# The expert stage's choice of width: compares in one block at the loop's head instead of a nested tree

## What is computed

```
top_val, top_idx = lax.top_k(tok @ w_router, 2)
xs = tok[token_of]                      # tokens sorted by expert
g = lax.ragged_dot(xs, w_gate, group_sizes)
u = lax.ragged_dot(xs, w_up, group_sizes)
y = lax.ragged_dot(jax.nn.silu(g) * u, w_down, group_sizes)
```

## Time and profile before

| what | value |
|---|---|
| device time, median of 3 runs | 4548.6 us (4547.06 to 4548.66) |
| span of the profiled execution | 4554.2 us |
| PE busy (share) | 3869.1 us (85%) |
| PEld busy | 3520.6 us (77%) |
| DVE / ACT / POOL busy | 2316.3 / 1755.4 / 829.9 us |
| expert stage, from its first product to the output phase | about 1795 to 4500 us |

### The profile page before, as it was taken

The page is one execution under the profiler, slowest core; times in us unless marked ns, Lnnn a source line. Parts: engine busy times, 40 slices in busy tenths (PEclk is TensorE's granted clock), DMA queues, the critical chain, the costliest instruction groups (busy, mean ns, idle before and its releaser), DMA issues. The chain is left out here.

```text
span 4554.2 us, 65309 instructions
## 1 busy us (share of the span) xinstructions
PE 3869.1 (85%) x23414; PEld 3520.6 (77%) x23415; DVE 2316.3 (51%) x3372; ACT 1755.4 (39%) x2324; POOL 829.9 (18%) x319
## 2 busy tenths in 40 slices
PE   5988867999999573869979979979699897997993
PEld 3964455777777452869979979978699897997993
DVE  2347733545545423756644444458444486454554
ACT  5146613322322132545433333345333354443442
POOL 0000000111111202322222112223222132221222
PEclk8988878999999786989989989999899998998996
DMA  4136634322322324655544444446443465444544
GB/s 166 34 131 222 222 105 171 102 92 92 108 95 65 140 113 98 225 174 185 184 129 133 138 137 135 134 154 229 138 154 132 135 221 178 157 138 137 175 166 178
DMA packets 433346, 662.95 MB, mean 146 GB/s; under 512 B 33361, under 2 KB 348881, under 8 KB 432977
## 3 DMA queue, kind: packets, MB, share of 16 engines
q1 hardware_dynamic: 413026, 587.84, 38.8%
q0 software_dynamic: 15776, 55.61, 3.4%
q10 hardware_dynamic: 4176, 15.21, 0.8%
HBM read 599.32 MB, written 59.29 MB: 145 GB/s over the span
## 5 line engine op out<-in xcount | busy, mean ns | idle before, releaser
L1822 POOL TENSOR_TENSOR moe_d_lo<-moe_raw_d,moe_d_hi 128x2048 fp32r<-128x2048 f32 x126 | 582.9, 4626 | 1947.3 <-ACT moe_d_hi L1962 1947.3
L2132 DVE SCALAR_TENSOR_TENSOR moe_y_t<-moe_y,moe_cols,moe_y_t 128x256 f32<-128x256 f32 (+3 forms) x936 | 480.7, 533 | 181.8 <-PE moe_y L1873 176.9
L1871 PE MATMUL moe_g<-moe_x,moe_g_hi 128*128 128x352 f32 (+3 forms) x1344 | 421.3, 313 | 145.0 <-issue 145.0
L2079 DVE TENSOR_TENSOR moe_g_lo<-moe_raw_g,moe_g_hi 128x2048 fp32r<-128x2048 f32 x127 | 359.2, 2829 | 214.2 <-ACT moe_g_hi L1962 212.9
L1872 PE MATMUL moe_g<-moe_x,moe_g_hi 128*128 128x352 f32 (+3 forms) x1344 | 421.0, 313 | 6.5 <-issue 6.5
L1873 PE MATMUL moe_g<-moe_x,moe_g_lo 128*128 128x352 f32 (+3 forms) x1344 | 420.1, 313 | 0.0
L1871 PE MATMUL moe_y<-moe_h,moe_d_hi 128*128 128x352 f32 (+3 forms) x1344 | 417.7, 311 | 1.3 <-DVE moe_y_t L2132 1.1
L1872 PE MATMUL moe_u<-moe_x,moe_u_hi 128*128 128x352 f32 (+3 forms) x1344 | 415.7, 309 | 0.0
L1872 PE MATMUL moe_y<-moe_h,moe_d_hi 128*128 128x352 f32 (+3 forms) x1344 | 415.7, 309 | 0.0
L1873 PE MATMUL moe_u<-moe_x,moe_u_lo 128*128 128x352 f32 (+3 forms) x1344 | 415.6, 309 | 0.0
L1873 PE MATMUL moe_y<-moe_h,moe_d_lo 128*128 128x352 f32 (+3 forms) x1344 | 415.5, 309 | 0.0
(11 more groups left out here) (317 smaller groups left out, 9509.7 us busy)
## 6 DMA issues: line engine op xcount, KB each, us to landing
moe_raw_g<-in_moe_w_gate SPq DMA_DIRECT2D x127, 1024.0 KB, 5.6
moe_raw_u<-in_moe_w_up SPq DMA_DIRECT2D x127, 1024.0 KB, 5.0
moe_raw_d<-in_moe_w_down SPq DMA_DIRECT2D x126, 1024.0 KB, 4.9
att_w_mod<-in_w_ada SPq DMA_DIRECT2D x20, 2048.0 KB, 8.6
scratch_y<-att_zeros SPq DMA_DIRECT2D x11, 2048.0 KB, 14.1
ffn_raw_g<-in_ffn_w_gate SPq DMA_DIRECT2D x22, 1024.0 KB, 5.5
ffn_raw_u<-in_ffn_w_up SPq DMA_DIRECT2D x22, 1024.0 KB, 5.4
ffn_raw_d<-in_ffn_w_down SPq DMA_DIRECT2D x22, 1024.0 KB, 4.9
```

The source lines that it names most:

```text
L1822: pool.tensor_tensor(d_lo[par][:, :, :], raw_d[:, :, :], d_hi[par][:, :, :].bitcast(F), ALU.subtract)\
L1871: pe.matmul(bank[:, 0:width], wh, moving[:, 0, 0:width], start=start, stop=False)
L2079: dve.tensor_tensor(lo[par][:, :, :], raw[:, :, :], hi[par][:, :, :].bitcast(F), ALU.subtract).then_inc(split, 1)
L2132: dve.scalar_tensor_tensor(y_t[:, db, 0:cols], y_ps[db % 4][:, 0:cols], gate, y_t[:, db, 0:cols], ALU.mult, ALU.add).then_inc(y_added, 1)
```

## The change

The head of the loop, all compares and the loop's end now lie in one block of some 22 instructions, ahead of all widths' programs. A compare jumps straight to a width's program, or falls to the next compare; the program of width 128 follows right behind the block. Each program ends with one jump to the loop's end (`tail`), which adds to the counter and jumps to `head`. Only when all 11 passes are done does the engine jump over all programs to the end of the stage. A pass without work goes from the first compare to the tail. SP, POOL and the dense layer keep `each_pass` or the plain list of passes. The loops inside a width's program and the work in it are the same; at the widths used they lie 3 to 13 instructions further on.

```
-        def each_width(eng, width_no, body):
+        def each_width(eng, who, body):
...
-            def among(first, last):
...
-                    width = WIDTHS[first - 1]
-                    body(width, 2 * width < TOKENS - 2 * ROUND)
...
-                with eng.If(width_no <= middle):
-                    among(first, middle)
-                    eng.nop()
-                with eng.If(width_no > middle):
-                    among(middle + 1, last)
-                    eng.nop()
...
+                with nc.body(node(first, last), valid_engines=this):
+                    if last - first > 1:
+                        eng.br_cond(width_no <= middle, on_true=node(first, middle), on_false=node(middle + 1, last))
+                    else:
+                        eng.br_cond(width_no <= first, on_true=node(first, first), on_false=f"{node(first, last)}_else")
...
+            nc.regs_mov(counter, 0)
+            nc.br(head, engines=this)
+            with nc.body(head, valid_engines=this):
+                p = nc.snap(counter, min_val=0, max_val=passes - 1)
+                width_no = eng.value_load(table[0:1, 1, bass.ds(p, 1)], min_val=0, max_val=len(WIDTHS))
+                eng.br_cond(width_no <= 0, on_true=tail, on_false=node(1, len(WIDTHS)))
+                tree(1, len(WIDTHS))
+                with nc.body(tail, valid_engines=this):
+                    nc.regs_add(counter, counter, 1)
+                    nc.br_lt(counter, passes, on_true=head, on_false=f"{end}_far", engines=this)
+                with nc.body(f"{end}_far", valid_engines=this):
+                    eng.br(end)
+                for k, width in enumerate(WIDTHS):
+                    with nc.body(node(k + 1, k + 1), valid_engines=this):
+                        body(p, width, 2 * width < TOKENS - 2 * ROUND)
+                        eng.br(tail)
+            nc.switch_bb(end)
...
-            each_pass(pe, one_pass)
+            each_width(pe, "pe", one_pass)
...
-            each_pass(act, one_pass)
+            each_width(act, "act", one_pass)
...
-            each_pass(dve, one_pass)
+            each_width(dve, "dve", one_pass)
```

More of the change, by code:

```diff
@@ L1723, in each_pass @@
                 for p in range(passes):
-                    body(p, None)
+                    body(p)
                 return
@@ L1728, in each_pass, with node, tree @@
                 with eng.If(width_no > 0):
-                    body(p, width_no)
+                    body(p)
                     eng.nop()
-        def each_width(eng, width_no, body):
-            if width_no is None:
-                body(TOKENS, False)
+        def each_width(eng, who, body):
+            if table is None:
+                for p in range(passes):
+                    body(p, TOKENS, False)
                 return
-            def among(first, last):
+            this = bass.OrderedEngineSet([eng.engine])
+            counter = nc.alloc_registers(f"{name}_{who}_pass", engines=this)
+            head, tail, end = (f"{name}_{who}_{at}" for at in ("head", "tail", "end"))
+            def node(first, last):
+                return f"{name}_{who}_widths_{first}_{last}"
+            def tree(first, last):
@@ L1753, in each_width @@
-            eng.nop()
+                with nc.body(node(first, last), valid_engines=this):
[3 more added lines that the diff above has]
+                        eng.br_cond(width_no <= first, on_true=node(first, first), on_false=f"{node(first, last)}_else")
+                if last - first == 1:
+                    with nc.body(f"{node(first, last)}_else", valid_engines=this):
+                        eng.br(node(last, last))
@@ new lines, in tree @@
+                tree(first, middle)
+                tree(middle + 1, last)
+            nc.regs_mov(counter, 0)
[14 more added lines that the diff above has]
+                        eng.br(tail)
@@ L1797, in expert_of, with one_pass @@
                 return sp.value_load(table[0:1, 0, bass.ds(p, 1)], min_val=0, max_val=gate_w.shape[0] - 1)
-            def one_pass(p, _):
+            def one_pass(p):
                 expert = expert_of(p)
@@ L2009, in ready_tokens @@
                     act.activation(x[:, k, 0, :], x_full[:, k % 2, :], ACT.Copy).then_inc(x_rounded, 1)
[L2011 to L2044, removed]
@@ new lines, in one_pass, with step @@
+            def one_pass(p, width, narrow):
+                def step(c, par, round_next=True):
+                    if round_next:
+                        round_g(p, c + 1, 1 - par)
+                    silu(p, c, 0, width, narrow)
+                    if round_next:
+                        round_u(p, c + 1, 1 - par)
+                    round_hidden(p, c, par, 0, width)
+                    silu(p, c, 1, width, narrow)
+                    round_hidden(p, c, par, 1, width)
+                    round_d(p, c, par)
+                chunk_pairs(act, p, 0, C - 2, step)
+                step(C - 1, parity(p, C - 1), has_next(p))
+                if has_next(p):
+                    ready_tokens(p + 1)
+                tiles = -(-width // P)
+                for t in range(TILES_PASS):
+                    if t < tiles:
+                        act.wait_ge(y_turned, p * KD + 2 * t + 1 + T0)
+                        act.wait_ge(y_stored[t % 2], (p * (TILES_PASS // 2) + t // 2 + 1) * 16)
+                        act.activation(y_out[:, t % 2, 0:D // 2], y_ps[2 * t % 4][:, :], ACT.Copy)\
+                           .then_inc(y_left, TILES_PASS - tiles + 1 if t == tiles - 1 else 1)
+                        act.wait_ge(y_left, p * TILES_PASS + t + 1 + O0)
+                        act.wait_ge(y_right, p * TILES_PASS + t + 1 + O0)
+                        act.dma_start(y_rows(p, t), y_out[:, t % 2, :]).then_inc(y_stored[t % 2], 16)
+                    else:
+                        act.wait_ge(y_stored[t % 2], (p * (TILES_PASS // 2) + t // 2 + 1) * 16)
+                        act.sem_inc(y_stored[t % 2], 16)
```

127 lines of the change are left out of this document (61 added, 66 removed).

## The result

The changed kernel takes 4413.6 us (4404.9 to 4422.4, four runs), the kernel before beside it 4548.6 (4547.1 to 4554.4): a ratio of 0.9706, 95% interval 0.9690 to 0.9721. That is 135 us less; 95 were forecast. A later comparison of the same two kernels (five and nine runs) gave 4416.8 against 4547.4, 130.6 us less, ratio 0.9706 (0.9693 to 0.9720). The direction held, the size did not, and the time lies outside the forecast range.

What follows compares the result with a forecast made beforehand. PE's idles between passes, 172.1 us of far-jump fetches, were taken as the bound; 91.0 us there plus 4.1 at the stage's end save 95.1, so 4554.2 becomes 4459.1, less 5.6 for the median: 4454 us, range 4440 to 4482.

Steps and rivals of the forecast that it cites:

- the block was not cut: Rival: a border between code pieces cuts the compact block, head and tail need a fetch each; 39 us less saved, 4493; chance 0.08.
- no inner loop fetched in its rounds: Rival, slower: a moved inner loop of ACT or DVE crosses a border and fetches each round; 216 us, 4670; chance 0.03.
- the exits of passes of width 128 and 160 were kept: PE's exits from narrow passes cost no fetch; the rival, every exit a fetch, 14.7 us less saved, 4469, chance 0.22.
- With one fetch I take 12.4 less 4.9 [...], 7.5 us.: PE's idle at a change with one fetch: the shortest earlier idle less the median jump back; after passes 0, 3, 4, 6.
- lost through the wide ones: PE's instruction memory loses the compact block during wide passes, so their exits fetch and four changes have two fetches.
- two fetches at 12.4: PE's idle at each of four changes with two fetches, taken as 12.4 us from an idle in the earlier trace.
- The end of the stage: ACT's way out after the last pass: exit, empty passes and one far jump, 4.1 us saved.
- ACT's corrections: Taken off PE's sum because ACT is late: 0.2 us at pass 1, 1.4 us after pass 3; 92.6 becomes 91.0.
- several us to spare: Outside passes 1 and 7 and the narrow passes, ACT was taken to have several us in hand before PE needs the weights.
- ACT sets the pace: Rival: ACT's walk paces every change, 17 fetches of 4 us, 68 + 4.1 us saved, 4477; chance 0.13.
- What else moves costs nothing: Counter, work in the programs, and order of SP's and POOL's loads and gathers stay the same; 0 us.
- The clock: PE's granted clock may stay up, or exits start earlier, at short idles: up to 2 us at four changes, 8 us, left out.

Runs made afterwards that it cites:

- tail_far: The changed kernel with PE's tail (count and jump back) behind all programs, as in the kernel before; 4453.5 us.
- exit_waits: The changed kernel, but PE's sequencer waits for its last transposes of a pass before it takes the exit; 4438.1 us.
- after_again: The changed kernel once more, unchanged; 4416.8 us, ratio 0.9706 to the kernel before.
- own_all: The changed kernel with a count, table read and compares of its own behind every program on PE, ACT and DVE; 4404.9 us, ratio 0.9684.

## Why the prediction was right in direction and wrong in size

**What held.** The idles are fetches at far jumps; tail_far puts ten more such fetches in and gets 44 us of idle and 40 us of time. The tail costs 0.2 us, the block was not cut, no inner loop fetched in its rounds, ACT did not set the pace, and the exits of passes of width 128 and 160 were kept. The terms of PE were the right terms: each of the eight idles shrank.

**The step that failed first: "With one fetch I take 12.4 less 4.9 [...], 7.5 us."** Measured are 4.46, 3.97 and 4.59 us after passes 0, 4 and 6, and 5.69 into the 128 of pass 4: 11.3 us over four changes. The 12.41 of the earlier trace rows is a poor measure in two ways. Taking off the jump back leaves in it the exit of 5.97 us, where entries after the change took 3.7 to 4.2 us in most changes. And its lead is as short as any: its first far jump starts 1.0 us ahead of the end of the transposes (3017.0, the idle beginning at 3018.0), while after the change the exits start 1.1 to 3.6 us ahead, and where the exit is kept all of the lead goes into the entry's fetch. I named this with "up to 2 us at four changes" and left it out of the sum. exit_waits prices the lead at 21.3 us over eight changes, 2.7 each; 1.0 of each was in my measure, so some 13 us over the eight were not, by this estimate.

**The second: the block "lost through the wide ones".** Behind passes 1 and 5 it was kept, so that two changes for which I took 12.4 us had 2.67 and 7.29, 14.8 us. I had reasoned from six packets in a wide pass and two at its entry. From the exit ahead of pass 1 to that after it the trace after shows 7 packets of q8; so it does through pass 2, whose exit was lost (windows 2006 to 2263 and 2265 to 2602.6 us). Through pass 5 (3173.1 to 3512) it was 4, presumably since part of 352's code was still there from pass 3. The rows of these three windows, and that of pass 0 (1785 to 2004.5):

```profile
q8 instruction: 7, 0.11, 0.2%
...
q8 instruction: 7, 0.11, 0.2%
...
q8 instruction: 4, 0.07, 0.1%
...
q8 instruction: 3, 0.05, 0.1%
```

The number of packets does not decide it alone. Counting every place as new in each wide pass was the error at pass 5.

**The third: two fetches at 12.4.** They were 10.53 and 10.07, and 11.2 in after_again: 4.2 us for the two. The three parts make 11.3 + 14.8 + 4.2 = 30.3, the 30.2 us that were missing.

**The end of the stage** gave 6.6 and not 4.1 us. **ACT's corrections** (0.2 at pass 1, 1.4 in the narrow passes) had the wrong place for the first: PE waited for the low parts 1.9 and 1.6 us in pass 4, where the 1.6 stood before the change as well, and 0.3 us in pass 2, and not at pass 1. That DVE hangs on ACT was read rightly, but that both have "several us to spare" elsewhere was true of the shortened walks only: with the old ones PE waits in seven passes. The rival "ACT sets the pace" was closer than its 0.13 says: it became true as soon as ACT kept its tree.

**"What else moves costs nothing"** did not hold either: the 6.5 us of second stops in the passes of 352 went away. It didn't show in the sum, since as much came back: the stage length less the idles is 2507.5 us before and 2506.9 after.

**The clock**, which I had left out: over the first 10 us of the eight passes the mean granted clock was 0.74 of full speed before and 0.79 after, part of it perhaps because the second stops were gone. The first product after the shortest idle (2.67 us) took 0.42 us instead of 0.66, the other seven took 0.57 to 0.66, much as before. No gain of the size that I allowed for is seen in the passes' own length.

The sum: the span lost 143.3 us and not 95.1. Of the 48.2 between them, 30.2 are PE's idles, 1.6 ACT's corrections that didn't come where I put them, 2.5 the end of the stage, 11.5 the chance ahead of the stage, and 2.4 the second stops (6.5) less what came back elsewhere (4.1). Without the chance 36.7 are left, and the longer comparison misses 35.5 (130.6 less 95.1).

## What to carry to other kernels

Price a far jump as a fetch, then subtract what the sequencer's lead and the waits around it cover, place by place: an idle taken from the place with the shortest cover overstates what will remain at the others. Where several engines walk the same branches side by side, shorten all the walks at once; one alone gives nothing or half (here 0 to 3, 65, and 131 to 135 us for ACT with DVE, for PE, and for all three). Putting a fetch ahead of work that others wait for only moves the idle; a copy of the choosing code behind each program removes the way back altogether.

## What the runs showed of the hardware that I had not expected

PE's instruction memory kept a block through programs of 256 and 352. Neither "oldest out" nor "longest unused out" with one fixed size fits what was seen. By age: the block came in anew at the exit of pass 2 and was lost at that of pass 3, 8 packets later; it came in anew there and was kept until the exit of pass 6, 15 packets later. By last use: 7 packets lay between two uses in pass 1, where it was kept, and 7 in pass 2, where it was lost. The first two counts (2609.5 to 2951.9 and 2957 to 3738 us):

```profile
q8 instruction: 8, 0.13, 0.2%
...
q8 instruction: 15, 0.25, 0.1%
```

The Trainium skill (Runtime: NRT & Kernel Launch, "Instruction fetch mechanics") describes PE's as a FIFO of 128 KiB filled in blocks of 16 KiB, which makes eight blocks, and beside it two cache lines. After the block at the head had come in, 3 packets came in pass 0 and 7 up to the exit of pass 1, ten in all, and that exit took 0.30 us; here the measurement speaks against both descriptions. What decides between keeping and losing stays open.

Kernels with the same work ahead of it reached the expert stage at times from 1779.4 to 1799.4 us in 17 profiled executions of 16 kernels, and the changed kernel itself at 1783.6 and 1791.9. This is a scatter of 0.4% of the time, more than most differences between the versions above, and only a length measured inside the stage tells them apart.

On ACT a far jump does not show in the branch. ACT's branches of the choice took 34 to 50 ns in the changed kernel, whether they led far or not, and the stop lies behind them as an idle put down to "issue". What one costs ACT is known only as a bound: in own_all, with a single way to walk, ACT's idle behind the passes of three tiles was 2.93, 5.45, 5.23 and 5.57 us (into passes 3, 4, 6 and 8).
